# Transposing keys and queries of an attention mixer in 32x32 squares and through DRAM, in a float32 decoder layer

## The reference, cut to what matters

```python
z = h @ w_in                                  # 2048 x 12288
q, k, v, u, ga, gc = split(z)                 # q, k, v: 16 heads of 128
scores = q_h @ k_h.T * 128 ** -0.5 - slope_h * (t - s), causal
o_h = softmax(scores) @ v_h
y_conv = silu(layer_norm(depthwise_conv31(a * sigmoid(g)))) @ w_conv_out
mix = (sigmoid(ga) * (o @ w_attn_out) + sigmoid(gc) * y_conv) @ w_out
```

## Time and profile before

| | |
|---|---|
| median of 3 runs | 2117.32 us (2117.18 to 2117.36) |
| the profiled execution | 2117.16 us |
| its span | 2115.3 us |
| granted TensorE clock, mean | 0.998 |
| PE busy | 2102.1 us, 99% |
| DVE busy | 1868.6 us, 88% |
| ACT busy | 1406.2 us, 66% |
| POOL busy | 194.2 us, 9% |
| HBM read, written | 529.93 MB, 16.78 MB |

### The profile page before, as it was taken

How to read it: one execution, slowest core, us unless ns; L and a number is a source line. 1 busy time by engine, 2 the same in 40 slices (tenths; PEclk the granted TensorE clock), 3 DMA queues, 4 the chain that set the end, 5 groups by cost and what they waited for, 6 DMA issues and landing times.

```text
span 2115.3 us, 23794 instructions
## 1 busy us (share of the span) xinstructions
PE 2102.1 (99%) x9420; PEld 1740.6 (82%) x9420; DVE 1868.6 (88%) x1404; ACT 1406.2 (66%) x1321; POOL 194.2 (9%) x305
## 2 busy tenths in 40 slices
PE   9999999999999999999999999999999999999998
PEld 7888888888888888888888888888888888888886
DVE  8899999999997889999899986659899999999996
ACT  6677777778775547666676435435677777777773
POOL 0111111100110000000000000000111111110110
PEclk9999999999999999999999999999999999999999
DMA  9688888898886759787888656755688888898883
GB/s 359 238 285 274 266 268 269 293 308 277 288 276 237 274 154 316 251 261 224 273 266 251 232 189 231 259 187 199 237 289 262 276 262 275 290 308 276 288 276 123
DMA packets 89709, 548.26 MB, mean 259 GB/s; under 512 B 12416, under 2 KB 12800, under 8 KB 32512
## 3 DMA queue, kind: packets, MB, share of 16 engines
q1 hardware_dynamic: 68544, 437.69, 54.5%
q0 software_dynamic: 21056, 109.07, 24.5%
HBM read 529.93 MB, written 16.78 MB: 258 GB/s over the span
## 4 chain that ended last, share of the span: by engine, by line
PE 99%; DMA 0%; DVE 0%; SPq 0%; ACT 0%; issue 0%; DVEq 0%
PE acc L2194 16%; PE acc L2196 16%; PE acc L2195 16%; PE tb L2194 12%; PE tb L2196 12%; PE tb L2195 12%; PE acc L2132 3%; PE acc L2134 3%; PE acc L2133 3%; PE tb L2180 1%; DMA g_raw<-in_groups 0%; PE tb L2475 0%; PE tb L2491 0%; PE tb L2492 0%; PE tb L2474 0%; DVE res L2035 0%
## 5 line engine op out<-in xcount | busy, mean ns | idle before, releaser
L1326 DVE TENSOR_TENSOR g_lo<-g_raw,g_hi 128x2048 fp32r<-128x2048 f32 x506 | 1147.3, 2285 | 136.5 <-ACT g_hi L804 136.1
L804 ACT ACTIVATE g_hi<-g_raw 128x2048 fp32r<-128x2048 f32 x506 | 964.7, 1916 | 343.3 <-DVE g_raw L1334 105.4
L2194 PE MATMUL acc<-g_hi,xF_hi 128*128 128x512 f32 x1216 | 477.9, 393 | 1.9 <-DVE g_lo L1653 1.3
L2196 PE MATMUL acc<-g_hi,xF_lo 128*128 128x512 f32 x1216 | 473.7, 390 | 0.0
L2195 PE MATMUL acc<-g_lo,xF_hi 128*128 128x512 f32 x1216 | 473.2, 389 | 0.0
L2194 PE MATMUL tb<-g_hi,xF_hi 128*128 128x512 f32 x760 | 297.1, 391 | 0.0
L2196 PE MATMUL tb<-g_hi,xF_lo 128*128 128x512 f32 x760 | 295.9, 389 | 0.0
L2195 PE MATMUL tb<-g_lo,xF_hi 128*128 128x512 f32 x760 | 295.7, 389 | 0.0
L1334 DVE TENSOR_TENSOR g_raw<-g_raw,g_raw 128x2048 f32<-128x2048 f32 x120 | 274.3, 2286 | 1.4
L2194 PEld LDWEIGHTS acc<-g_hi,xF_hi 128*128 128x128 f32 x1216 | 228.3, 188 | 50.3 <-DVE g_lo L1653 2.6
L2196 PEld LDWEIGHTS acc<-g_hi,xF_lo 128*128 128x128 f32 x1216 | 228.3, 188 | 48.2
(11 more groups left out here) (169 smaller groups left out, 2243.5 us busy)
## 6 DMA issues: line engine op xcount, KB each, us to landing
g_raw<-in_groups SPq DMA_DIRECT2D x356, 1024.0 KB, 7.0
g_raw<-in_groups POOLq DMA_DIRECT2D x80, 1024.0 KB, 8.3
raw<-in_stream SPq DMA_DIRECT2D x80, 512.0 KB, 4.7
bounce<-h_sq POOLq DMA_DIRECT2D x40, 256.0 KB, 5.0
h_in<-bounce POOLq DMA_DIRECT2D x160, 64.0 KB, 2.8
ln_gb<-in_ln SPq DMA_DIRECT2D x6, 1024.0 KB, 6.9
g_raw<-in_groups SPq DMA_DIRECT2D x6, 512.0 KB, 9.1
res<-in_x_rows SPq DMA_DIRECT2D x1, 2048.0 KB, 16.0
```

Of the source, the lines that this page charges most:

```text
L804: act.activation(g_hi[:, n % RING], source[:], ACT.Copy).then_inc(g_hi_ready, 1)
L1326: dve.tensor_tensor(g_lo[:, n % RING], source[:], f32(g_hi[:, n % RING]), ALU.subtract).then_inc(g_lo_ready, 1)
L2194: pe.matmul(bank, x_hi_ap, g_hi[:, n % RING, blk], start=begin, stop=False, skip_group_check=True)
L2196: return pe.matmul(bank, x_lo_ap, g_hi[:, n % RING, blk], start=False, stop=end, skip_group_check=True)
```

## The change

- `turn_k` and `turn_q` and their ScalarE copies go. In mixing block g, after the low half of P1b, VectorE transposes the 32 x 32 squares of the keys of block g-1 from `k_sb` into `kT` (new layout: 4 x 2 x 4 x 32 per partition), after the low half of Q1 those of the queries into `q_sq`.
- GpSimd writes the key squares (512 KB) to `k_bounce`, then issues the accumulating transfer of T1b, then reads the keys back into `kT` in four transfers; the same follows for the queries, by `q_bounce` into `q_sq`; only then comes the accumulating transfer of T3b. Five transfers per operand.
- ScalarE, behind the split of P6a (which moves ahead of this), waits for the queries and copies them to `qT` in two instructions.
- `scores` of heads 0 and 1 move from after Q2 to after P5b, those of heads 2 and 3 from after P5b to after P6a; each head takes three products of 128 columns, not one of 128 and one of 256.
- Taps: blocks 1 to 4 have 16, now (0, 0, 0, 0, 2, 2, 3, 3, 3, 3); before 3 in the first two places and 3 in the fifth, 1 elsewhere (block 4: 23 in all). Each piece of the gate chunks has one more.
- First chunk: each part runs its high-high and low-high products as soon as the part's high half is made, and only its high-low products wait for the low half; 10 warm-up matmuls, not 12.
- First block of FFN 1: `factor_lo` 2 and 3 go behind the first sum, and the sum onto `ra` becomes an accumulating transfer. FFN 2 keeps the addition.
- The space for descriptors of GpSimd's transfers goes from 1024 to 2048 bytes; `stats` moves to another place in SBUF.

```diff
-WARM = 12
+WARM = 10
...
-BLOCK_TAPS = ((1, 3), (1, 3), (1, 3), (1, 3), (2, 3), (2, 1))
+HEAD_TAPS = (0, 0, 0, 0, 2, 2, 3, 3, 3, 3)
+BLOCK_TAPS = ((3, 3, 1, 1, 3, 1, 1, 1, 1, 1), *([HEAD_TAPS] * NG), (1, 1, 2, 2, 1, 2, 2, 2, 2, 2))
...
+    k_bounce = nc.dram_tensor("k_bounce", (QD, STEP, QD, TT, BLK, STEP), F32, kind="Internal").ap()
+    q_bounce = nc.dram_tensor("q_bounce", (QD, STEP, QD, TT, BLK, STEP), F32, kind="Internal").ap()
...
-                split_sum(f, b, "P7", "ra", "T3")
+                if f:
+                    split_sum(f, b, "P7", "ra", "T3")
+                else:
+                    act.wait_ge(t3_first, 16)
+                    split(f, b, "P7", "ra")
...
-            def heads_of(dst, g, first):
-
-                for t in range(TT):
-                    act.wait_ge(tr_full, turned(g) + first + t + 1)
-                    act.activation(dst[:, :, t * P:(t + 1) * P], tb[:, t].rearrange("p (b n) -> p b n", b=HG),
-                                   ACT.Copy).then_inc(qk_ready, 1)
-
-            def keys_turned(g):
-                heads_of(kT, g, 0)
-
             def queries_turned(g):
+
+                act.wait_ge(q_loaded, 16 * QD * (g + 1))
                 if g:
                     act.wait_ge(o_stored, 16 * g)
-                heads_of(qT, g, 2)
+                for t in range(TT):
+                    act.activation(qT[:, :, t * P:(t + 1) * P].rearrange("p b (a n) -> p a b n", a=QD), q_sq[:, :, t],
+                                   ACT.Copy).then_inc(qT_ready, 1)
...
-                if heads:
-                    keys_turned(g - 1)
-                elif g == 0:
+                if g == 0:
                     conv_block(1)
                 fork(f, g, acc[:, BY], acc[:, BX], "P1b")
                 act.wait_ge(t1b_ready, fulls(f, g))
                 split(f, g, "P5b", "qb")
+                split_sum(f, g, "P6a", "qa", "T2a")
                 if heads:
                     queries_turned(g - 1)
-                split_sum(f, g, "P6a", "qa", "T2a")
                 split_loaded(f, g, "P3a", "ua")
...
-                load_done(f, b, "ua")
-                dve.wait_ge(t_ready, G.sum_no[f, b, "T1"])
-                add(ra, ra, ua)
+                if f:
+                    load_done(f, b, "ua")
+                    dve.wait_ge(t_ready, G.sum_no[f, b, "T1"])
+                    add(ra, ra, ua)
+                else:
+                    factor_lo(f, 2)
+                    factor_lo(f, 3)
+                    load_done(f, b, "ua")
...
+            def square(dst, src, squared_one):
+
+                dve.transpose(dst.rearrange("p c b n -> p b c n"),
+                              src.rearrange("p (b c n) -> p b c n", b=BLK, c=QD)).then_inc(squared_one, 1)
+
+            def keys_squared(g):
+
+                for t in range(TT):
+                    dve.wait_ge(k_out, 2 * g + t + 1)
+                    square(kT[:, :, t], k_sb[:, t], k_squared)
+
+            def queries_squared(g):
+
+                dve.wait_ge(k_squared, TT * (g + 1))
+                for t in range(TT):
+                    dve.wait_ge(q_out, 2 * g + t + 1)
+                    square(q_sq[:, :, t], act_sb[:, t], q_squared)
...
                 lo_group(f, g, "P1a", "qa")
                 lo_group(f, g, "P1b", "qb")
+                if heads:
+                    keys_squared(g - 1)
                 split_done(f, g, "P1a")
                 load_done(f, g, "ra")
                 add(qa, qa, ra)
                 lo_group(f, g, "Q1", "Q1")
                 if not g:
                     conv_value(1)
-                taps(some)
+                if heads:
+                    queries_squared(g - 1)
+                taps(counts[0])
...
+            def squares_out(g, squared_one, squares, dram, sent):
+
+                pool.wait_ge(squared_one, TT * (g + 1))
+                pool.dma_start(dram.rearrange("a p c t b n -> (a p) (c t b n)"),
+                               squares.rearrange("p c t b n -> p (c t b n)")).then_inc(sent, 16)
+
+            def heads_in(g, sent, dst, dram, loaded_all):
+
+                pool.wait_ge(sent, 16 * (g + 1))
+                for c in range(QD):
+                    pool.dma_start(dst[STEP * c:STEP * (c + 1)].rearrange("p a t b n -> p a (t b n)"),
+                                   dram[:, :, c].rearrange("a p t b n -> p a (t b n)")).then_inc(loaded_all, 16)
+
             def mixing_sums(g):
 
                 f = "mix"
+                if 0 < g <= NG:
+                    squares_out(g - 1, k_squared, kT[:], k_bounce, k_sent)
                 pool.wait_ge(g_lo_ready, lo_count(G.at[f, g, "P1b"]))
                 add_from_hbm(f, g, "qb", "rb", t1b_ready)
+                if 0 < g <= NG:
+                    heads_in(g - 1, k_sent, kT[:], k_bounce, kT_loaded)
+                    squares_out(g - 1, q_squared, q_sq[:], q_bounce, q_sent)
+                    heads_in(g - 1, q_sent, q_sq[:], q_bounce, q_loaded)
...
-                pe.wait_ge(qk_ready, 4 * g + 4)
                 if pair:
                     pe.wait_ge(s_ready, HG * g + 2)
+                else:
+                    pe.wait_ge(kT_loaded, 16 * QD * (g + 1))
+                    pe.wait_ge(qT_ready, TT * (g + 1))
+                    if g:
+                        pe.wait_ge(o_ready, 2 * g)
+                    else:
+                        pe.wait_ge(ch_ready, 4)
                 for h in (2 * pair, 2 * pair + 1):
-                    pe.matmul(tb[:, h % 2, 0:P], qT[:, h, 0:P], kT[:, h, 0:P], start=True, stop=True)
-                    pe.matmul(tb[:, h % 2, P:SC], qT[:, h, P:T], kT[:, h, :], start=True, stop=True).then_inc(tr_full, 1)
+                    pe.matmul(tb[:, h % 2, 0:P], qT[:, h, 0:P], kT[:, :, 0, h], start=True, stop=True)
+                    pe.matmul(tb[:, h % 2, P:2 * P], qT[:, h, P:T], kT[:, :, 0, h], start=True, stop=True)
+                    pe.matmul(tb[:, h % 2, 2 * P:SC], qT[:, h, P:T], kT[:, :, 1, h], start=True,
+                              stop=True).then_inc(tr_full, 1)
...
-                if heads:
-                    turn_k(g - 1)
                 if g:
                     pe.wait_ge(q_out, 2 * g)
                 else:
                     turn_conv(1)
                 query_group(g, 0)
-                if heads:
-                    turn_q(g - 1)
                 query_group(g, 1)
-                if heads:
-                    scores(g - 1, 0)
                 if g:
                     pe.wait_ge(v_out, 2 * g)
                 else:
...
                 product_group(f, g, "P5a", W, S1, 0, begin=True)
                 product_group(f, g, "P5b", W, S1, 1)
                 if heads:
-                    scores(g - 1, 1)
+                    scores(g - 1, 0)
                 wait_fork(f, g, 0)
                 product_group(f, g, "P6a", X, S2, 0)
+                if heads:
+                    scores(g - 1, 1)
...
-                    pe.wait_ge(part_lo, h + 1)
+                    pe.wait_ge(part_hi, h + 1)
+                    if h in (0, 4, 6):
+                        pe.wait_ge(x_hi, (0, 4, 6).index(h) + 1)
+                    for t in range(TT):
+                        for blk in range(first, last):
+                            high_only(banks[g % 2][t], piece(p, t)[0][:, blk], g, blk, p == 0 and blk == 0)
                     if h in (0, 4, 6):
                         pe.wait_ge(x_lo, (0, 4, 6).index(h) + 1)
                     for t in range(TT):
                         for blk in range(first, last):
-                            mm = mm3(banks[g % 2][t], piece(p, t)[0][:, blk], piece(p, t)[1][:, blk], g, blk,
-                                     p == 0 and blk == 0, False)
+                            high_only(banks[g % 2][t], piece(p, t)[1][:, blk], g, blk, False)
+                    pe.wait_ge(part_lo, h + 1)
+                    for t in range(TT):
+                        for blk in range(first, last):
+                            mm = high_low(banks[g % 2][t], piece(p, t)[0][:, blk], g, blk)
...
+            pool.wait_ge(t_ready, G.sum_no[0, 1, "T1"])
+            add_from_hbm(0, 1, "ra", "ua", t3_first)
```

More of the change, by code:

```diff
@@ L154, in __init__ @@
                     rows += 1
-                for name in FULL_SUMS if is_full(b) else HALF_SUMS:
+                for name in FULL_SUMS if is_full(b) else HALF_SUMS[f]:
                     sums += 1
@@ L355, in build @@
         ident = place("ident", [P, P])
-        stats = place("stats", [P, TT, ND, 6])
         mv = place("mv", [P, TT, 2])
@@ L394, in build @@
         k_sb = place("k_sb", [P, TT, COLS], at=pr_at)
+        q_sq = place("q_sq", [P, QD, TT, BLK, STEP], at=pr_at)
         gate_q = place("gate_q", [P, TT, COLS], at=res_at + 4 * HG * T)
@@ L431, in build @@
         t1b_ready = sem("t1b_ready")
+        t3_first = sem("t3_first")
         t3b_ready = sem("t3b_ready")
@@ L475, in build @@
         conv_step = sem("conv_step")
-        qk_ready = sem("qk_ready")
+        k_squared = sem("k_squared")
```

(34 more changed lines are left out.)

28 lines of the change are left out of this document (8 added, 20 removed).

## The result

The changed kernel takes 2132.78 us (median of 4 runs, 2130.78 to 2134.09), the kernel before 2117.27 (2117.18 to 2117.36). The ratio is 1.0072, 95% interval 1.006 to 1.0085: 0.7% slower, 15.5 us, where 2110.9 was forecast and 2108.4 to 2117.8 was the range. The profiled execution took 2134.09 us, its span is 2132.3.

What follows compares the result with a forecast made beforehand. TensorE was taken to bound the kernel, busy 68.71 of 68.71 us in a mixing block. 2117.16 - 7.07 (transposes) - 1.25 (first chunk) + 2.0 (wait before P7a) = 2110.9 us; range 2108.4 to 2117.8.

Steps and rivals of the forecast that it cites:

- Transposes off TensorE: Mixing blocks 1 to 4: removing key and query transposes saves 0.884 us per episode, eight episodes, 7.07 us.
- The start: First chunk: the new product order lets TensorE enter the fifth part 1.25 us earlier; bounds 0 and 1.4.
- the forecast cover of 0.7 us: First chunk, plain group 4: low half ready at 28.1, TensorE there at 28.8, so the whole 1.25 us is kept.
- The new wait in front of P7a: Mixing blocks: three groups, not four, before P7a, which needs X's save; 0.5 us per block, 2.0 in all.
- own lateness: Before P7a: VectorE's delay, added with hand-overs to S+9.6 against TensorE's S+9.5 to take 0.5 us per block.
- Arrival, 17.5: Mixing block: the queries' last read lands 17.5 us after the block's first product, in order of GpSimd's queue.
- My upper end, 22: Mixing block: the latest landing of the queries, with both writes at 8.3 us: 5.5+8.3+8.3=22.
- What lateness costs: Mixing blocks: queries up to +18 cost nothing; each us later costs each of four blocks 1 us.
- Taps "at nothing": Block 4 gives 7 taps of 0.4 us each to the gate chunks, priced at no cost.
- rival 2: Mixing blocks: queries past +21, TensorE waits at the first scores too; arrival-18 per block, 2127 at +22; chance 0.11.
- Rival 1: Mixing blocks: queries at 19 to 20.1 through queue order, 1 to 2.1 us more per block, 2115 to 2119; chance 0.19.
- the cover to 18: Mixing block: the queries may land until 18 us after the block's first product without TensorE losing time.

Runs made afterwards that it cites:

- The start alone: The kernel before with only the edits to first chunk, warm-up and first FFN block: 2116.27 us against 2117.47.
- The run without the accumulate: The changed kernel with T1b's 1 MB accumulating transfer in blocks 1 to 4 cut to 8 KB, so its result differs: 2112.55 us, one execution.
- the taps back: The changed kernel with the taps' move undone: block 4 has its seven taps again, the gate pieces 5 or 7: 2129.96 us.
- the plain transfer: The changed kernel with T1b in blocks 1 to 4 a 1 MB transfer without adding, same place in the queue, so its result differs: 2121.96 us.
- the mirror: The changed kernel with the keys transposed by TensorE as before and the queries over DRAM, taps still moved: 2115.60 us.
- the best kernel here: The changed kernel with the queries transposed by TensorE, the keys over DRAM and the taps' move undone: 2112.50 us, ratio 0.9978.

## Why the prediction was wrong

**Transposes off TensorE, 7.07 us: right.** 0.87 us for one episode in a block, 1.78 for two. The strided keys and the three 128-column products cost nothing that can be seen. (A block before is 68.48 us from first product to first product, not 68.71, whose window ends one product late; VectorE's cover in it was 0.2 us less than the prediction had. And its sum, added up, is 2110.84.)

**The start, 1.25 us: right** (1.34 at block 1, 1.2 in the median). At plain group 4 the forecast cover of 0.7 us wasn't there: its low half ended at 28.74, 0.6 later than forecast, and TensorE waited 0.43 us. The start alone has no such wait and comes to block 1 just as early.

**The new wait in front of P7a, 2.0 us in four parts: wrong.** The run without the accumulate has the scores in the same places and no such wait; in the changed kernel it comes once, 1.8 us in block 4, behind queries that were late. That this is near 2.0 is chance. Why only block 4 has it isn't shown; the runs with the taps back and with the plain transfer have it there too (1.4 and 1.9). The step that added VectorE's "own lateness" to a difference of 0.1 us made a term out of nothing.

**Arrival, 17.5: the step that failed**, and in it one term. The accumulate was to land at +8.5 and did at +9.2. The keys' four reads behind it were given 1.5 us (to +10) and took 6.8, landing at +11.1, 12.9, 14.4 and 16.0. The queries' write behind them was given 3 and took 2.2 (+18.2), their reads 4.5 and took 4.8 (+23.0). So, by the order of landings, 5.3 of 5.5 us are the keys' reads: 512 KB priced by a median of 64 KB reads over the whole kernel, in a stretch where two 1 MB loads of SyncE's were on the way (issued 831.94 and 835.33, landed 842.73 and 846.87). My upper end, 22, was built of two slow writes; it left out slow reads, and the true value lay beyond it.

**What lateness costs: right.** No loss at +18.4 (without the accumulate) and +18.3 (the mirror), 2.28 us at +20.9, 4.38 at +23.0, 5.84 at +24.5 (the taps back, block of 72.78 for 66.94). That is a limit of 18.5 and 0.95 to 0.97 us per us, where 18 and 1 were forecast. Blocks 3 and 4 lost over 6 us for two reasons. In block 3 the queries came at +24.4, which by this rate is 5.7, and the clock fell. In block 4 they came at +22.9, which is 4.2, and the rest is the wait at P7a.

**Taps "at nothing": wrong.** No cover was named for the gate chunks. Eight pieces with 0.4 us more each make VectorE, and by it SyncE's loads and `attn_rows`, about 3 us later: 3.94 us in the profiled execution, 2.8 in the median.

**The rival.** What happened is rival 2, slower by arrival past 21, to which I gave 0.11. By its own rule at +23: 2110.9 + 4 x 5 = 2130.9; without the P7a term and with the taps 2132.8. That this meets the median so closely is luck, since the rule has neither the clock nor a later block 3. Rival 1 named order in the queue as the mechanism, from what the Trainium skill says of rings (DMA: Bandwidth & Descriptors, section "Queues, rings and completion order"). That was part of it: the queries' write landed 2.8 us earlier from a queue of its own and 5.1 earlier ahead of the accumulate. It wasn't enough, since the reads behind it then ran beside an accumulate, and both kernels were slower. What decides is how much is in flight ahead of the queries' landing, in any queue.

**Where it should have been seen.** GpSimd's queue moved in block 1 of the kernel before 4.74 MB for 34.7% of the engines' time, SyncE's 12.59 MB for 47.2% (DMA table, 830 to 899: packets, MB, share of 16 engines); in the changed kernel (829 to 900) GpSimd's is

```profile
q0 software_dynamic: 1392, 6.82, 42.7%
```

From 24 us to 30 for 2.1 MB more: 6 us of all 16 engines. The prediction priced each transfer by its own time to landing and never summed what the engines were given. That sum, an estimate from the table of before: T1b at 5.0 us per MB, two loads and the 1.6 MB of trips up to the queries' write at 2.6 make 14.8 us. Counted from the keys' write at -1.4, the queries' write can't land before +13.4, and with 4.5 us for the reads they arrive at +17.9 if nothing is left over from earlier loads. So it would have shown that the cover to 18 was gone, and that every slow row falls on the far side; it wouldn't have given +23. The free time of before wouldn't have shown it either: 3.7 us in the window of 0.08, and 5 more from T3b, which moved away, against 4.5 us for the trips.

## What to carry to other kernels

Before work is moved to DMA, read the DMA share in windows as short as the wait that you must meet, not as a mean over the block. Then list what is in flight when your transfer goes out, in all queues, price it at the row's own us per MB, and see whether it ends before the due time. A free window behind that doesn't help, and full engines don't hurt what isn't due: the best kernel here is full from its block's start to +28. Where the list is too long, take something off it (half of this change is worth 4.9 us, the whole costs 15.5). Moving entries about within it only moved the wait: both runs that did so were slower. And a queue that waits may be what keeps its next transfer out of a full stretch.

## What the runs showed of the hardware

Adding while transferring is dear: 1 MB from DRAM onto SBUF took 10.1 us with adding and 6.5 without, in the same place of the same queue. By the tables it is 24 us for 4.74 MB (5.0 us per MB of all 16 engines, nearly all of them accumulates) against 33 us for 12.59 MB of plain loads (2.6).

TensorE's granted clock fell behind some waits. Behind the 2.06 us its products come every 0.43 us and not 0.227, for some 3 us, which is the lower of its two levels (1.2 GHz). So a wait of 2.1 us cost 3.9. At this place waits of 1.1, 1.4, 1.6 and 1.6 us left the clock at 1.00, and those of 1.9, 2.1, 2.2 and 2.4 were followed by the lower level. But the length of a wait doesn't settle it: at the scores it stayed full behind 2.39 us, and in the run with the taps back behind 3.84. The timeline of the changed kernel at `attn_out`:

```profile
1242.69 0.39 PE L2187 MATMUL acc<-w_hi,oT_lo 128*128 128x512 f32 x1
1245.13 0.80 PE L2185 MATMUL acc<-w_hi,oT_hi 128*128 128x512 f32 x1 [2.06 <-DVE sig_a L1941]
1245.72 0.63 PE L2186 MATMUL acc<-w_lo,oT_hi 128*128 128x512 f32 x1
...
1247.86 0.63 PE L2185 MATMUL acc<-w_hi,oT_hi 128*128 128x512 f32 x1
...
1248.64 0.39 PE L2187 MATMUL acc<-w_hi,oT_lo 128*128 128x512 f32 x1
```
